# The order of the token tiles in the selected attention of a two-block transformer kernel

## What is computed

```python
# sliding window: query t sees keys s with 0 <= t - s < 128, with a sink per head
o_b = swa_branch(b_q, b_k, b_v, sinks)
# selected attention: an indexer scores all causal keys, each query keeps its top 128
_, sel = lax.top_k(score, topk)
logits = einsum(q, k[sel]) * scale, masked to sel <= qpos
o_a = softmax(logits) @ v[sel]
mix = sigmoid(g_a) * (o_a @ w_branch_a) + sigmoid(g_b) * (o_b @ w_branch_b)
x = x + mix @ w_out_2
```

## Time and profile before

| what | value |
|---|---|
| time, median of 3 runs | 1676.07 us (1675.97 to 1676.46) |
| the profiled execution's own time | 1677.33 us |
| its span, first to last instruction | 1675.5 us |
| PE busy | 1620.2 us (97%) |
| DVE, ACT, POOL busy | 774.1, 491.4, 799.6 us |
| mean granted TensorE clock | 0.989 |
| slots 32 to 70 and the wait for `y_a` | 1157.94 to 1236.90 us of the span |

### The profile page before, as it was taken

How to read it: one execution, slowest core, us unless ns; L and a number is a source line. 1 busy time by engine, 2 the same in 40 slices (tenths; PEclk the granted TensorE clock), 3 DMA queues, 4 the chain that set the end, 5 groups by cost and what they waited for, 6 DMA issues and landing times.

```text
span 1675.5 us, 19583 instructions
## 1 busy us (share of the span) xinstructions
PE 1620.2 (97%) x7556; PEld 1339.4 (80%) x7556; DVE 774.1 (46%) x1076; ACT 491.4 (29%) x735; POOL 799.6 (48%) x304
## 2 busy tenths in 40 slices
PE   7999999999998999999998999979999899999998
PEld 5887788888887888888886887867878788888886
DVE  6701588800555666664005488954452632013202
ACT  3012211200003434333123244245542343123312
POOL 5874287777876444444446003411135444434442
PEclk9999999999999999999998999989999999999999
DMA  5332033332233233332221322210022132232221
GB/s 201 101 126 75 3 105 101 101 101 84 92 101 101 76 101 100 99 90 93 95 101 59 99 79 72 80 51 26 26 76 101 52 99 101 101 101 95 89 97 72
DMA packets 123280, 147.47 MB, mean 88 GB/s; under 512 B 5142, under 2 KB 98374, under 8 KB 123206
## 3 DMA queue, kind: packets, MB, share of 16 engines
q1 hardware_dynamic: 121622, 141.90, 26.2%
q10 hardware_dynamic: 1584, 4.52, 0.8%
HBM read 144.31 MB, written 2.10 MB: 87 GB/s over the span
## 4 chain that ended last, share of the span: by engine, by line
PE 87%; DVE 7%; POOL 3%; issue 1%; ACT 1%; DMA 0%; SPq 0%; DVEq 0%; POOLq 0%; ACTq 0%
PE ps L582 26%; PE ps L583 26%; PE ps L584 26%; PE ps L691 2%; DVE work L1649 2%; PE ps L921 2%; PE ps L761 2%; DVE top L1646 2%; PE ps L907 2%; POOL w_lo L526 1%; DVE h_rows L1340 1%; POOL w_hi L517 1%; PE ps L818 1%; PE ps L749 1%; DMA raw<-in_w_in 0%
## 5 line engine op out<-in xcount | busy, mean ns | idle before, releaser
L526 POOL TENSOR_TENSOR w_lo<-raw,w_hi 128x1024 fp32r<-128x1024 f32 (+1 forms) x246 | 617.8, 2533 | 694.4 <-ACT w_hi L965 690.9
L582 PE MATMUL ps<-hT_hi,w_hi 128*128 128x512 f32 (+1 forms) x960 | 371.4, 387 | 1.0 <-DVE hT_lo L1351 0.5
L584 PE MATMUL ps<-hT_hi,w_lo 128*128 128x512 f32 (+1 forms) x960 | 368.2, 384 | 0.0
L583 PE MATMUL ps<-hT_lo,w_hi 128*128 128x512 f32 (+1 forms) x960 | 368.2, 384 | 0.0
L517 POOL TENSOR_TENSOR w_hi<-raw,cells 128x2048 fp32r<-128x2048 f32 x45 | 168.2, 3739 | 158.9 <-PE ps L582 158.9
L965 ACT ACTIVATE w_hi<-raw 128x2048 fp32r<-128x2048 f32 (+1 forms) x85 | 161.0, 1895 | 247.9 <-PE ps L582 246.2
L582 PEld LDWEIGHTS ps<-hT_hi,w_hi 128*128 128x128 f32 x960 | 181.9, 189 | 36.8 <-POOL w_lo L526 1.4
L584 PEld LDWEIGHTS ps<-hT_hi,w_lo 128*128 128x128 f32 x960 | 181.7, 189 | 35.4
L583 PEld LDWEIGHTS ps<-hT_lo,w_hi 128*128 128x128 f32 x960 | 181.8, 189 | 34.3 <-issue 0.2
L583 PE MATMUL ps<-w_lo,f_hi 128*128 128x512 f32 x432 | 170.2, 394 | 0.0
L582 PE MATMUL ps<-w_hi,f_hi 128*128 128x512 f32 x432 | 169.3, 392 | 0.0
(11 more groups left out here) (258 smaller groups left out, 2128.7 us busy)
## 6 DMA issues: line engine op xcount, KB each, us to landing
raw<-in_w_in SPq DMA_DIRECT2D x86, 512.0 KB, 4.6
raw<-in_w_up SPq DMA_DIRECT2D x76, 512.0 KB, 4.5
raw<-in_w_down SPq DMA_DIRECT2D x54, 512.0 KB, 4.1
raw<-in_w_out SPq DMA_DIRECT2D x16, 512.0 KB, 4.1
raw<-in_w_ret_o SPq DMA_DIRECT2D x8, 512.0 KB, 4.5
raw<-in_w_sgu_o SPq DMA_DIRECT2D x8, 512.0 KB, 4.4
x<-in_x SPq DMA_DIRECT2D x4, 512.0 KB, 7.5
raw<-in_w_branch_b SPq DMA_DIRECT2D x4, 512.0 KB, 4.4
```

Source lines behind the costliest of these rows:

```text
L526: nc.gpsimd.tensor_tensor(w_lo[:, s, c], raw[:, s, c], w_hi[:, s, c].bitcast(f32), ALU.subtract).then_inc(unit_split, 1)
L582: first = nc.tensor.matmul(dst, a_hi, b_hi, start=start, stop=False)
L583: nc.tensor.matmul(dst, a_hi, b_lo, start=False, stop=False)
L584: return first, nc.tensor.matmul(dst, a_lo, b_hi, start=False, stop=stop)
```

## The change

One table. `TILE[turn]` of the turns 4 to 7 becomes 0, 1, 2, 3 where it was 3, 2, 1, 0. All three engines take the tile from this table, so the logits, transposes, copies, values and the place where a turn's output is written follow it. The slot numbers of the parts, of the weights' rounding, of `oTb_hi` and `oTb_lo`, and every buffer stay as they are.

```diff
 PAIRS = 2 * NT * HEADS
-TILE = [0, 1, 2, 3, 3, 2, 1, 0]
+TILE = [0, 1, 2, 3, 0, 1, 2, 3]
 GA_IN = KT // 2
```

## The result

| | before | after |
|---|---|---|
| median of 14 runs | 1676.45 us | 1679.87 us |
| profiled execution, its span | 1677.33, 1675.5 us | 1680.43, 1678.6 us |
| slot 32's logits to the start of `y_a` | 78.96 us | 82.49 us |
| PE busy | 1620.2 us | 1621.2 us |

The ratio is 1.0021, with a 95% interval of 1.0012 to 1.0029: 3.4 us slower, between 2.0 and 4.9. The forecast was +2.4 us, with 1676.3 to 1682.8 as its range. The measured centre lies right at the edge of what can be told from no change, where I had 0.29 for slower and 0.68 for the same. Among all the executions in this document one was slow (2043 us at a granted clock of 0.75, of the kernel with the order 3, 2, 0, 1); it is in that kernel's median and not in its ratio.

A forecast was written before the change was run, and what follows sets the result against it. TensorE was taken as the bound, with time changing only through its waits or clock. Waits of 7.4 or 7.5 us against 5.1 gave +2.4 us on the median 1676.07: 1678.5 us, range 1676.3 to 1682.8.

The forecast's parts named there:

- The bound: Slot 32 to `y_a`: TensorE busy 74.88 of 78.96 us, other engines under half busy; time changes only through TensorE's waits or clock.
- The chain: Odd heads' values wait on logits, softmax, exponential, copy: for tile 0, 1.68 us against 0.83 of TensorE work.
- What the long slots gain: From slot 48 on, waits fall from 3.5 to 1.1 us; slot 59's weight rounding and the gate products cost nothing.
- Slot 32: Start of the changed stretch, at 1157.94 us; no wait was forecast in this slot.
- The clock: Slots 33 to 45: some 11 us of work in 17, gaps of at most 1.3 us; granted clock holds at 1.00.
- its rival: Somewhere from slot 36 to 45 the clock falls to 1.2 GHz: 4.2 us more, +6.6 in all, 1682.7 us; chance 0.15.
- the row that I took for a likeness: Trace from 15 to 20 us: TensorE busy 3.52 of 5 us at granted clock 1.00, taken as similar to slots 33 to 45.
- the sum: All waits from slot 32 to `y_a`: 7.4 or 7.5 us against 5.1 before, +2.4 us; chance 0.66.
- The tail and the rest: Wait before `y_a` stays 1.7 us, parts 30 and 31 cover VectorE's scaling; slot 46's part does not wait for `oTb_lo`.
- The two halves of the count: Waits up to slot 47: 6.3 us, before 1.7; from slot 48 on: 1.1 us, before 3.5.
- The sign of 0.9 us a slot in the turn of tile 0: Sign of being right: from slot 36 on, the turn of tile 0 takes about 0.9 us a slot.

The follow-up runs named there:

- The exchange on ScalarE: ScalarE copies probabilities of head s-3 before the exponential of head s: 1675.12 us on the changed kernel, 1673.25 us on the kernel before.
- the exchange there: VectorE also copies head s-3 before its work for head s, on top of ScalarE doing so: 1672.05 us with changed order, 1670.4 with order of before.
- the two fills: Changed kernel with three 64-column products before values of odd heads 31 to 41: 1678.81 us; with twelve transposes instead: 1679.94 us.

## Why the prediction was right, and where its sizes were off

**The bound.** TensorE was taken as the bound, with the time only in its waits. The work and the busy time stayed, the waits grew; that step held.

**The chain.** The waits forecast from logits, softmax, exponential, copy and values were met to 0.2 us at slots 35, 37, 41, 43, 45 and 49. The exchange on ScalarE shows the chain as the cause, not only as a description: breaking it at one place took 4.8 us from the changed kernel. That ScalarE was short of time in the short slots has fallen with it, and VectorE likewise: the exchange there took 3.1 us more, with its work unchanged. In slots 37 and 45 VectorE's end of a turn is a link of the chain, as forecast: softmax 36 starts at 1164.50, 1.36 us after the late values of head 31.

**What the long slots gain.** I counted 2.4 us as saved from slot 48 on (3.5 to 1.1); measured it is 2.8 (3.5 to 0.7): the rounding of weights at slot 59 and the gate products cost nothing beside tile 3, and slot 55 and the drain cost even less than I gave them. The exchange of tiles 0 and 1 agrees: where tile 0 stands beside the parts did not matter.

**Slot 32.** Here I had no wait, and 0.4 us was measured. It is the same kind of chain, on VectorE: the copy of head 28 stands behind softmax 31 and, at the turn's end, the addition of line 1708, and starts at 1157.95 in the changed kernel. Before, the 512-wide logits of slot 32 hid it; the 128-wide ones don't. I had followed only the odd heads there.

**The clock.** This step failed in its likeliest case, and the size of its rival was wrong too. I expected the clock to hold, because 15 to 20 us into the kernel it held with TensorE busy 3.52 of 5 us; in the changed kernel it fell behind 2.42 of 3.72 us. That the waits made it fall is shown by the two fills. Why just there is not, and the busy share alone does not say it, since right behind the dip, with waits of 1.30 and 1.12 us in slots 41 and 43, it held with less (columns as in the earlier trace rows):

```profile
1170.00:1175.00 5.00, 2.91 (x18) 2.09 (x17) 3.59 (x12) 4.00 (x14) 0.00 (x0) 1.00 0.00 0
```

So the row that I took for a likeness proved nothing either way. As rival I gave the fall 4.2 us; it was 0.9 to 1.0. The low clock lasted 4 us, where I had reckoned with 6, and in that time TensorE would have waited 0.9 us anyway (slot 39), which the slower work swallowed: 1.8 lost in place of 0.9. No wait became longer by it. That the time stayed near the sum although this rival, with its chance of 0.15, came true is luck: its price was four times too large. The Trainium skill ("TensorE: Matmul & The Clock Gate", the section on psum-queue depth-cycling) tells of a kernel with short idles between groups of matmuls whose clock went down and up. The measurement agrees in that a fall came behind two short waits; the waits of slots 41, 43 and 45, two of them longer, brought none. That page's section on PE-mode transpose says that transposes don't count as busy in the same way; with transposes as the fill the clock held at 1.00, so here they did as well as products did. Real products stood around them in both, so the runs don't show what transposes alone would do.

**The tail and the rest.** The wait in front of `y_a` was the same, 1.72 us in the bracket (1.75 in the kernel filled with transposes); no part waited for `oTb_lo`.

**Slips in the working.** 0.53 + 0.39 + 0.40 + 0.31 is 1.63 and not 1.68, so slots 35 and 39 were given 0.05 too much each. The turns 6 and 7 have ten parts and not eleven. The two halves of the count (6.3 less 1.7, and 1.1 less 3.5) give +2.2, and the +2.4 comes from rounded totals. The sign of 0.9 us a slot in the turn of tile 0 doesn't fit its own waits of 1.1 and 0.9 us: slots 36 to 39 took 1.1 us each with the clock held by the fill, and 1.3 in the changed kernel.

**The sum.** +2.4 was forecast and +3.4 measured: 0.4 from slot 32, 0.9 from the clock, 0.4 less from slot 48 on, and 0.3 unassigned make 3.6 with it, against 3.5 in the stretch. Each is smaller than the width of the measured interval (2.0 to 4.9), so the sum is confirmed better by the slots of the profile than by the times. The chances were less good than the sum: with two unknowns that could only add, the clock and waits not followed, the mass should have been nearer to one half for slower.

## What to carry to other kernels

In a pipeline of events that several engines walk in one order, price each hand-over as a chain from the instruction that starts it to the one that needs it, and set it against what the waiting engine has to issue in between: a busy share of 48% on the helpers said nothing here. Short steps need independent work of the waiting engine inside that chain, in front of the instruction that waits; behind it, it covers nothing. And before moving work between steps, look at the order within one engine's step: doing the copy that is wanted now before the work that is wanted three steps later gave 6 us, almost twice what the tile order had cost.

## What the runs showed of the hardware

TensorE's clock fell to 1.2 GHz without any long idle stretch: two waits of 0.67 and 0.95 us, 2.4 us apart, with TensorE busy 2.42 of 3.72 us, were followed by 4 us at the low clock, at the same place in two executions. Three products of 64 columns in each wait kept it at 2.4 GHz. Waits of 1.30, 1.12 and 0.91 us a few microseconds later left it at 2.4 GHz; what tells the two places apart these runs don't show.

A VectorE addition of 8 columns with both inputs in SBUF took 1.72 us while GpSimd ran a subtraction of 1024 columns, and ended with it, against 0.17 us alone, while the softmax ahead of it, which reads PSUM and a table in SBUF, took its usual 0.48. In the kernels with the exchanges the same addition took 1.13 to 1.48 us beside a subtraction, and ended within 0.05 us of it each time, while a copy out of PSUM beside a subtraction took its usual 0.29. The Trainium skill ("GPSIMD Engine Reference", key points) tells of such a contention for VectorE instructions with two SBUF inputs; the trace agrees.
